# Stationary matmul tiles stored in pairs, element by element, instead of one after the other

## What is computed

```python
proj = u @ w_in[l]
...
mix = jnp.concatenate([h, y], axis=-1) @ w_out[l]
...
up = causal_dwconv(u @ ffn_up[l], ffn_conv_w[l], ffn_conv_b[l])
a, gt = jnp.split(up, 2, axis=-1)
f = (jax.nn.silu(gt) * a) @ ffn_down[l]
```

## Time and profile before

| | |
|---|---|
| three runs | 2200.99, 2202.62, 2195.91 us, median 2200.99 |
| the profiled execution | 2200.18 us, of which the span of the trace is 2198.1 us |
| granted clock of PE, mean | 0.994 |
| busy share | PE 97%, PEld 78%, POOL 68%, DVE 51%, ACT 30% |
| moved by DMA | 215.98 MB, mean 98 GB/s |

### The profile page before, as it was taken

The page is one execution under the profiler, slowest core; times in us unless marked ns, Lnnn a source line. Parts: engine busy times, 40 slices in busy tenths (PEclk is TensorE's granted clock), DMA queues, the critical chain, the costliest instruction groups (busy, mean ns, idle before and its releaser), DMA issues.

```text
span 2198.1 us, 26833 instructions
## 1 busy us (share of the span) xinstructions
PE 2138.4 (97%) x9588; PEld 1709.5 (78%) x9588; DVE 1117.0 (51%) x1982; ACT 663.2 (30%) x1142; POOL 1498.2 (68%) x741
## 2 busy tenths in 40 slices
PE   7999999999999999999999999999999999999997
PEld 3878777768888887788868888886788777888886
DVE  6899974884444103777643222105877835222101
ACT  3413335123222103444442111104555534111100
POOL 5868575667777887644379777886333348877785
PEclk9999999999999999999999999999999999999999
DMA  6323223732333332222123333332222222333332
GB/s 247 107 84 96 77 78 106 268 142 96 95 95 96 105 105 86 80 84 78 48 76 106 96 97 99 102 106 83 59 67 68 68 68 77 96 96 98 102 105 86
DMA packets 56371, 215.98 MB, mean 98 GB/s; under 512 B 6216, under 2 KB 6216, under 8 KB 53088
## 3 DMA queue, kind: packets, MB, share of 16 engines
q1 hardware_dynamic: 52992, 206.96, 29.3%
q10 hardware_dynamic: 3296, 7.91, 1.1%
HBM read 212.70 MB, written 2.15 MB: 98 GB/s over the span
## 4 chain that ended last, share of the span: by engine, by line
PE 78%; DVE 10%; POOL 4%; ACT 3%; issue 3%; DMA 2%; SPq 0%; DVEq 0%; POOLq 0%; ACTq 0%
PE ps L371 63%; DVE y L2036 3%; PE ps L603 2%; PE ps L1192 2%; DMA raw<-in_wstream 2%; PE ps L408 2%; POOL w_hi L974 1%; POOL w_lo L980 1%; PE ps L1284 1%; PE ps L1130 1%; PE ps L1315 1%; PE ps L1421 1%; PE ps L1302 1%; ACT u_hi L476 1%; DVE u_lo L526 1%
## 5 line engine op out<-in xcount | busy, mean ns | idle before, releaser
L980 POOL TENSOR_TENSOR w_lo<-raw,w_hi 128x1024 fp32r<-128x1024 f32 x335 | 813.6, 2429 | 199.3 <-ACT w_hi L1879 175.5
L974 POOL TENSOR_TENSOR w_hi<-raw,ones 128x1024 fp32r<-128x1024 f32 x304 | 582.9, 1918 | 368.9 <-DMA raw<-in_wstream 368.3
L371 PE MATMUL ps<-u_hi,w_hi 128*128 128x512 f32 x1760 | 708.9, 403 | 7.1 <-DVE qk L2047 2.8
L371 PE MATMUL ps<-u_hi,w_lo 128*128 128x512 f32 x1760 | 687.9, 391 | 0.0
L371 PE MATMUL ps<-u_lo,w_hi 128*128 128x512 f32 x1760 | 686.5, 390 | 0.0
L371 PEld LDWEIGHTS ps<-u_hi,w_hi 128*128 128x128 f32 x1760 | 332.1, 189 | 77.2 <-issue 6.7
L371 PEld LDWEIGHTS ps<-u_hi,w_lo 128*128 128x128 f32 x1760 | 331.1, 188 | 71.2
L371 PEld LDWEIGHTS ps<-u_lo,w_hi 128*128 128x128 f32 x1760 | 331.9, 189 | 66.9 <-issue 3.6
L371 PE MATMUL ps<-f_hi,w_lo 128*128 128x512 f32 x528 | 205.4, 389 | 0.0
L371 PE MATMUL ps<-f_hi,w_hi 128*128 128x512 f32 x528 | 205.4, 389 | 0.0
L371 PE MATMUL ps<-f_lo,w_hi 128*128 128x512 f32 x528 | 205.4, 389 | 0.0
(11 more groups left out here) (366 smaller groups left out, 2901.4 us busy)
## 6 DMA issues: line engine op xcount, KB each, us to landing
raw<-in_wstream SPq DMA_DIRECT2D x342, 512.0 KB, 3.6
ada_buf<-in_ada SPq DMA_DIRECT2D x16, 1024.0 KB, 7.3
ada_start<-in_ada SPq DMA_DIRECT2D x8, 1024.0 KB, 17.0
cbc<-decay_rows ACTq DMA_DIRECT2D x7, 512.0 KB, 3.5
x<-in_xT SPq DMA_DIRECT2D x1, 2048.0 KB, 8.0
bc<-gate_rows ACTq DMA_DIRECT2D x4, 512.0 KB, 5.3
out_T<-x ACTq DMA_DIRECT2D x8, 256.0 KB, 2.2
prm<-in_params SPq DMA_DIRECT2D x1, 357.5 KB, 2.9
```

The costliest lines, as they stand in the source:

```text
L371: last = nc.tensor.matmul(out, a, b, start=(start and k == 0 and i == 0), stop=(stop and k == nk - 1 and i == 2))
L974: g.tensor_tensor(w_hi[slot][:], raw[slot][:], ones[:, 0:1].to_broadcast([P, D]), ALU.mult).then_inc(chunk_hi, 1)
L980: g.tensor_tensor(w_lo[slot][:], raw[slot][:], w_hi[slot][:].bitcast(f32), ALU.subtract).then_inc(chunk_split, 1)
```

## The change

Two neighbouring contraction tiles k and k+1 are no longer stored one after the other, as 128 floats and 128 floats, but alternately: element i of the first, element i of the second, and so on. This holds for the rounded and for the low weights. POOL and ACT read `raw` in the old order and write in the new one; PE reads a tile with a step of two floats (8 bytes). Because low weights written in that order would run over bytes of `raw` that have not been read yet, `raw` now begins 512 bytes behind the low weights of its slot instead of at the same address. That takes 2 KB more of each partition, and `low_rows` moves into bytes that the attention stage had left free.

```diff
-    raw = [place(f"raw{i}", D) for i in range(SLOTS)]
-    w_lo = [nc.alloc_sbuf_tensor_at(f"w_lo{i}", [P, D], f32r, offset=here[0] - (SLOTS - i) * 4 * D) for i in range(SLOTS)]
+    raw, w_lo = [], []
+    for i in range(SLOTS):
+        w_lo.append(nc.alloc_sbuf_tensor_at(f"w_lo{i}", [P, D], f32r, offset=here[0]))
+        here[0] += 4 * P
+        raw.append(place(f"raw{i}", D))
...
+    def high_of(slot, k):
+        return w_hi[slot][:, k // 2 * 2 * P + k % 2:(k // 2 + 1) * 2 * P:2]
+
+    def low_of(slot, k):
+        return w_lo[slot][:, k // 2 * 2 * P + k % 2:(k // 2 + 1) * 2 * P:2]
+
+    def by_pairs(t, cols=slice(0, D)):
+        return t[:, cols].rearrange("p (j s i) -> p j s i", s=2, i=P)
+
+    def interleaved(t, cols=slice(0, D)):
+        return t[:, cols].rearrange("p (j i s) -> p j s i", s=2, i=P)
...
-            wh, wl = w_hi[slot][:, k * P:(k + 1) * P], w_lo[slot][:, k * P:(k + 1) * P]
+            wh, wl = high_of(slot, k), low_of(slot, k)
...
-            g.tensor_tensor(w_hi[slot][:], raw[slot][:], ones[:, 0:1].to_broadcast([P, D]),
+            g.tensor_tensor(interleaved(w_hi[slot]), by_pairs(raw[slot]), one_by_pairs(D),
                             ALU.mult).then_inc(chunk_hi, 1)
...
-            g.tensor_tensor(w_lo[slot][:], raw[slot][:], w_hi[slot][:].bitcast(f32),
+            g.tensor_tensor(interleaved(w_lo[slot]), by_pairs(raw[slot]), interleaved(w_hi[slot]).bitcast(f32),
                             ALU.subtract).then_inc(chunk_split, 1)
...
-            A(w_hi[c % SLOTS][:], raw[c % SLOTS][:], ACT.Identity).then_inc(chunk_hi_act, 1)
+            A(interleaved(w_hi[c % SLOTS]), by_pairs(raw[c % SLOTS]), ACT.Identity).then_inc(chunk_hi_act, 1)
```

More of the change, by code:

```diff
@@ L222, in build @@
     va_both = place("va_both", 8 * P, f32r, [2, NT, P])
-    low_rows, weighed = place("low_rows", T), place("weighed", T)
+    weighed = place("weighed", T)
     pt_hi = [place(f"pt_hi{i}", NT * T, f32r, [NT, T]) for i in range(2)]
@@ L231, in build @@
     pr = [place(f"pr{i}", T) for i in range(2)]
+    low_rows = place("low_rows", T)
     assert here[0] <= mix_end
@@ L390, in gemm_first @@
         for k in range(KT):
-            weights = [[w[(chunk + g) % SLOTS][:, k * P:(k + 1) * P] for w in (w_hi, w_lo)] for g in range(GROUP)]
+            weights = [[of((chunk + g) % SLOTS, k) for of in (high_of, low_of)] for g in range(GROUP)]
             high_wait(k)
@@ L624, in finish @@
             k = KT - 1
-            weights = [[w[(self.base + n) % SLOTS][:, k * P:(k + 1) * P] for w in (w_hi, w_lo)] for n in range(self.width)]
+            weights = [[of((self.base + n) % SLOTS, k) for of in (high_of, low_of)] for n in range(self.width)]
             if self.kept:
@@ L969, in _, with one_by_pairs @@
             q_n0.did(g.tensor_tensor(acc[:], sq[0][:] if n == 1 else acc[:], sq[n % 2][:], ALU.add), f"sq{n}")
+        def one_by_pairs(n):
+            return ones[:, 0:1].to_broadcast([P, n]).rearrange("p (j s i) -> p j s i", s=2, i=P)
         def split(c, slot, landed, rounded):
             pool.wait_ge(raw_landed[slot], landed)
-            g.tensor_tensor(w_hi[slot][:], raw[slot][:], ones[:, 0:1].to_broadcast([P, D]),
+            g.tensor_tensor(interleaved(w_hi[slot]), by_pairs(raw[slot]), one_by_pairs(D),
                             ALU.mult).then_inc(chunk_hi, 1)
@@ L998, in split_halves @@
                 cols = slice(h * D // 2, (h + 1) * D // 2)
-                high = g.tensor_tensor(w_hi[slot][:, cols], raw[slot][:, cols], ones[:, 0:1].to_broadcast([P, D // 2]), ALU.mult)
+                high = g.tensor_tensor(interleaved(w_hi[slot], cols), by_pairs(raw[slot], cols), one_by_pairs(D // 2), ALU.mult)
                 if h == 0:
@@ L1005, in split_halves @@
                     pool.wait_ge(chunk_hi, c + 1 - taken(c))
-                rest = g.tensor_tensor(w_lo[slot][:, cols], raw[slot][:, cols], w_hi[slot][:, cols].bitcast(f32), ALU.subtract)
+                rest = g.tensor_tensor(interleaved(w_lo[slot], cols), by_pairs(raw[slot], cols), interleaved(w_hi[slot], cols).bitcast(f32), ALU.subtract)
                 if h == 0:
@@ L1189, in wout_pe @@
                 hi, lo = (y_hi, y_lo) if half else (u_hi, u_lo)
-                wh, wl = w_hi[c % SLOTS][:, k * P:(k + 1) * P], w_lo[c % SLOTS][:, k * P:(k + 1) * P]
+                wh, wl = high_of(c % SLOTS, k), low_of(c % SLOTS, k)
                 for i, (a, b) in enumerate(tri(wh, wl, hi[:, k, :], lo[:, k, :])):
@@ L1791, in _ @@
                     act.wait_ge(chunk_split, C_FOXOUT + 1)
-                    for j, w in enumerate((w_hi, w_lo)):
-                        ins = A(last_row[:, j, :], w[C_FOXOUT % SLOTS][:, (KT - 1) * P:KT * P].bitcast(f32), ACT.Identity)
+                    for j, of in enumerate((high_of, low_of)):
+                        ins = A(last_row[:, j, :], of(C_FOXOUT % SLOTS, KT - 1).bitcast(f32), ACT.Identity)
                     a_fg.did(ins, "last_row")
```

## The result

The changed kernel takes a median of 2239.5 us (2237.0 to 2240.2), the kernel before, measured beside it, 2199.4 us (2195.9 to 2202.6). The ratio is 1.0181, 95% interval 1.0162 to 1.0200: **slower by 40 us**, where 72 us faster was forecast. The profiled execution took 2236.97 us, its span is 2235.0 us, 36.9 us more than before.

A forecast was written before the change was run, and what follows sets the result against it. PE's matmul pace was taken as the bound; -71 and -8 us for PE, +2 and +5 for POOL gave -72 us on 2200.2, so 2128 us (2129 for the median), range 2093 to 2295, the forecast's own 2093 to 2181.

The forecast's parts named there:

- PE's part: Matmuls with rounded or low weights: strided loads bring the pace from 226.7 to 216.0 ns, 71 us less on the path.
- the comparison row: Plain f32 matmuls of L343, which load 128 stationary columns too and pay 2.7 ns each over their columns.
- the 10.7 ns that f32 doesn't pay: Part of each fp32r matmul's 13.4 ns loss, read as load and moving stream hindering each other; taken as removed.
- meets the other stream differently: PE's weight load at twice the step moves twice as fast through memory beside the matmul's moving stream; 10.7 ns taken as removed.
- The 13.4 ns that were to go: What each fp32r matmul takes over its 512 columns' 213.3 ns; at best all goes, 108 us less.
- The loss stays: Rival on PE: the loss belongs to switching weights in fp32r form, whatever their addresses; 2201 to 2206 us, chance 0.22.
- The load touches twice the memory: Rival on PE's weight loads: twice the stretch doubles 13.4 to 26.8 ns, pace 240 ns, 2290 us; chance 0.11.
- POOL becomes the bound: Rival: POOL's strided streams raise a chunk to 5.62 us, above PE's time; 2294 us, chance 0.14.
- POOL's terms in the sum: POOL's strided read costs +0.40 us per chunk on low weights: 2 us in down projections, 5 us where POOL is uncovered.
- The 7 us counted for it (2 and 5): POOL's added time: 2 us in the down projections, 5 us where POOL itself stands in the chain.
- 68.3% of the chain: Share of four matmul lines, 1501 us or 6620 matmuls, each taken to gain 10.7 ns, 71 us in all.
- the prediction's 2.7 ns: What each plain f32 matmul of L343 was said to take over two passes of its columns.

The follow-up runs named there:

- e4: Groups of 16 matmuls, each with one form of operands, put behind the end of the kernel before; gaps 227 ns at step 1, 233 ns at step 2.
- e6: The changed kernel's layout with everything contiguous and all weight tiles starting four floats later; 2234.2 us, ratio 1.0144 to the kernel before.
- e7: The changed kernel with 192 bytes left free behind the rounded weights, moving its activations; 2225.1 us, ratio 1.0125.
- e9: The kernel before with 64 bytes left free behind the rounded weights, moving its activations; 2212.8 us, ratio 1.0063.
- e2: The changed kernel with POOL and ACT writing interleaved but PE reading contiguously; 2202.4 us, ratio 1.0016 to the kernel before.

## Why the prediction was wrong, step by step

**The step that failed** is the one that priced PE's part: "I take the value of the comparison row, the 10.7 ns that f32 doesn't pay, as removed". It is +6.6 ns instead of -10.7. The row it leaned on could not tell: plain f32 takes 429 ns at steps 1, 2 and 4 alike, so it says nothing about what a step does beside an fp32r matmul. What the two rows do show held: the loss belongs to fp32r. That it needs a moving operand at full rate is not shown; in e4 one read at half the rate (step 2) took 452 ns, 25 over two passes of its columns. That a strided load "meets the other stream differently" fits e6, e7 and e9; that different means better was a guess, and the guess had no row. Of 64 contiguous starts four give 226.7 ns, the kernel before used one of them, and there was more to lose than to win.

The 13.4 ns that were to go have a floor that no address removed. Settled at start 0, 256, 384 and 512 columns take 120.0, 173.3 and 226.7 ns, each 13.3 ns over its columns at 2.4 GHz (448 to 504 columns: 15.7 to 16.7), and none of the 64 starts at step 1 or the 26 at step 2 goes under it at 512 columns. Addresses only add to this floor, 6.6 ns in the changed kernel. What makes the floor stays open: every matmul of these runs has a load of its own.

**"The loss stays"** was nearer than the forecast: the floor behaves like the fixed price it names. But it counted the even pace as a sign of a price blind to addresses, and the even pace is a settled pattern: other starts settle as evenly at 230.0 or 233.3. The Trainium skill's rule beside it (SBUF — State Buffer, Who interferes with whom: independent read ports, PE waits on no one) would, read so, make the pace blind to where the operands lie. e6 and e9 contradict that reading for fp32r: addresses alone moved the kernel by 1.4% and 0.6%.

**"The load touches twice the memory"** had the sign and the place, and 26.8 ns over the columns where 20.0 was measured. Its mechanism is refuted, not only its size: with a load that touches one float (step 0) the pace is 230 ns, with a contiguous one that starts 16 bytes on 233.3, and step 2 costs nothing extra at 384 columns.

**"POOL becomes the bound"** did not happen (PE's longest wait for POOL is 2.3 us, 2.9 before), and POOL's terms in the sum were too high: +0.40 us on the low weights was +0.04. The rule quoted from the Trainium skill (GPSIMD Engine Reference, Performance pitfalls for Q7 kernels), no cliff up to a step of 8 bytes, agrees with 2429 to 2471 ns. The 7 us counted for it (2 and 5) compare with 3 us in e2. No wait of PE is put down to ACT's `w_hi`: those writes stayed covered.

**The path.** 68.3% of the chain was taken as matmuls that gain or lose fully. It is right for the feed-forwards, 4440 of the 6620. The other 2180 would have lost 14 us at 6.6 ns each; the span has 7.4 us left for them. Outside the feed-forwards a matmul lost less: over all gaps of consecutive weight matmuls under 245 ns, those in runs of more than 150 went from 226.7 to 233.3 ns, the shorter runs from 229.1 to 233.4. In the gated recurrence the chain has runs of nine between small matmuls, before:

```profile
1662.53 2.08 PE ps L371 x9
...
1665.05 2.08 PE ps L371 x9
```

and after:

```profile
1658.69 2.10 PE ps L387 x9
...
1666.95 2.12 PE ps L387 x9
```

That is 231 ns each before and 233 to 236 after: runs so short had not settled at 226.7 in the first place, so they had less to lose. By the starts of the chain's pieces, 2.9 of the 7.4 us arose ahead of the first feed-forward, 3.2 between the first and the second, and 1.4 in the stage shown here, ahead of the third.

**The range** missed nothing on its upper side (2239 lies between 2093 and 2295); the direction and the likeliest case were wrong.

## What to carry to other kernels

A stream of matmuls that runs at full rate beside its weight loads can have a pace that hangs on where the two operands start; when such a kernel's time changes by a per cent or so after buffers were moved, divide the unbroken pieces of the chain by their counts before looking anywhere else. A comparison row of another data type bounds a price, but does not give the sign of an edit; a probe of some 24 matmuls with the very operand form does, and its settled pace carried over to the unbroken stretches of the kernel to 0.2 ns (16 matmuls were too few at step 1: 229 ns in the first group). Look for a floor first: the 13.3 ns that stood at 256, 384 and 512 columns alike were not to be had by any start. Keep weight and activation tiles at equal distance in every slot and tile, so that one measured start holds everywhere.

## What the runs showed of the hardware that was not expected

- Paces favour a few values: 41 of the 64 starts give 226.7, 230.0 or 233.3 ns, which are 544, 552 and 560 cycles of 2.4 GHz for 512 columns; 173.3 ns is 416 for 384 columns, 120 ns is 288 for 256. What sets these values, and why step 0 pays as much as a load of 128 floats, no run here settles.
- The load's own time jumps with the step: 188, 193, 252, 310 and 332 ns at steps 1, 2, 3, 4 and 8. At step 4 the pace is 233 to 235 ns with 256, 384 and 512 columns alike, so there the load, not the columns, sets it. The Trainium skill (SBUF — State Buffer, Door 1: The DMA port swizzle) tells of 16-byte lines that want at least two hits each; step 2 still has two floats in a line, step 4 one, and the jump of the loads agrees. The same note of the Trainium skill calls steps of up to 4 fp32 free, and here the measurement differs: 310 ns at step 4, and twice the time for a moving operand with step 2. The step-0 row, 184 ns, gave no hint of it.
- A moving operand with a step of two floats goes at half the rate: 452 ns for 512 columns (step 1 weights) in e4.
- In the probe, 16 plain f32 matmuls leave 32 records at 429 ns each, so a row of L343 is half a matmul of the program, and the prediction's 2.7 ns is the price of such a half.
